# Token sums of a mixture-of-experts stage split over three places of TensorE's order, on Trainium2

## What is computed

```python
def block_mlp(args):
    xb, e = args
    return (jax.nn.silu(xb @ w_gate[e]) * (xb @ w_up[e])) @ w_down[e]
...
y_pad = y_pad * w_pad[:, None].astype(y_pad.dtype)
out = jax.ops.segment_sum(y_pad, tok_pad, num_segments=n_tok)
```

## Time and profile before

| | |
|---|---|
| median of three runs | 2187.53 us (2187.5 to 2188.99) |
| the profiled execution | 2186.75 us, span 2184.9 us |
| TensorE busy over the span | 2123.9 us (97%) |
| VectorE busy | 1211.1 us (55%) |
| ScalarE busy | 855.5 us (39%) |
| mean granted TensorE clock | 0.995 of full speed |
| from the first matmul of expert 0's `gate_up` to that of expert 31's | from 1709.33 us to 2156.12 us |

### The profile page before, as it was taken

One profiled execution on the slowest core, in us unless ns is written; L12 is line 12 of the kernel. 1 busy time (PEld: TensorE's weight loads), 2 busy tenths in 40 slices (PEclk: granted clock), 3 DMA queues, 4 the chain that ended last, 5 costly groups with the idle time before them and its releaser, 6 DMA issues.

```text
span 2184.9 us, 29571 instructions
## 1 busy us (share of the span) xinstructions
PE 2123.9 (97%) x12238; PEld 1521.8 (70%) x12238; DVE 1211.1 (55%) x1983; ACT 855.5 (39%) x1385; POOL 221.1 (10%) x301
## 2 busy tenths in 40 slices
PE   7999999999999999999999999999999899999998
PEld 6868757877777777898888888888867433333333
DVE  3532972439888867875423466345443445544454
ACT  4325461468886544672332542334443111111112
POOL 2000000013331022562000000000001000000000
PEclk9999999999999999999999999999999999999999
DMA  7122112423322444201222221433446899999994
GB/s 249 59 74 93 46 39 83 127 87 97 97 77 94 164 127 154 92 22 41 94 80 97 97 97 40 135 108 123 135 174 243 330 420 420 420 420 420 421 420 194
DMA packets 115703, 366.60 MB, mean 168 GB/s; under 512 B 7952, under 2 KB 36944, under 8 KB 90352
## 3 DMA queue, kind: packets, MB, share of 16 engines
q1 hardware_dynamic: 105888, 329.34, 40.2%
q0 software_dynamic: 9168, 29.00, 3.9%
q10 hardware_dynamic: 512, 6.34, 0.7%
HBM read 358.44 MB, written 10.54 MB: 169 GB/s over the span
## 4 chain that ended last, share of the span: by engine, by line
PE 88%; DVE 8%; ACT 2%; issue 1%; DMA 0%; POOL 0%; SPq 0%; DVEq 0%; ACTq 0%; POOLq 0%
PE bank L956 39%; PE bank L1167 13%; PE bank L1711 10%; PE bank L1725 5%; PE bank L1733 3%; PE bank L1284 2%; PE bank L1180 2%; PE bank L1211 2%; DVE resid L3369 2%; PE bank L1276 1%; PE bank L1113 1%; PE bank L1701 1%; PE bank L1104 1%; DVE w_lo L2447 1%; PE bank L1073 1%
## 5 line engine op out<-in xcount | busy, mean ns | idle before, releaser
L2447 DVE TENSOR_TENSOR w_lo<-raw,w_hi 128x2048 fp32r<-128x2048 f32 x117 | 268.6, 2296 | 444.1 <-ACT w_hi L1842 443.9
L1842 ACT ACTIVATE w_hi<-raw 128x2048 fp32r<-128x2048 f32 x117 | 223.9, 1914 | 393.9 <-PE bank L956 357.5
L3369 DVE TENSOR_TENSOR resid<-bank,resid 128x512 f32<-128x512 f32 x244 | 151.1, 680 | 182.6 <-PE bank L1733 182.6
L956 PE MATMUL bank<-hT_hi,w_hi 128*128 128x512 f32 x512 | 199.9, 390 | 2.5 <-DVE y_lo L3065 2.3
L956 PE MATMUL bank<-hT_lo,w_hi 128*128 128x512 f32 x512 | 199.2, 389 | 0.0
L956 PE MATMUL bank<-hT_hi,w_lo 128*128 128x512 f32 x512 | 199.2, 389 | 0.0
L1711 PE MATMUL bank<-piece,xT 128*64 128x512 f32 x792 | 183.4, 592 | 0.0
L1167 PE MATMUL bank<-hT_hi,w_hi 128*128 128x512 f32 x432 | 173.9, 402 | 0.9 <-DVE hT_lo L2511 0.9
L1167 PE MATMUL bank<-hT_hi,w_lo 128*128 128x512 f32 x432 | 168.2, 389 | 0.0
L1167 PE MATMUL bank<-hT_lo,w_hi 128*128 128x512 f32 x432 | 168.1, 389 | 0.0
L1711 PEld LDWEIGHTS bank<-piece,xT 128*64 128x64 f32 x792 | 59.5, 137 | 118.8 <-issue 118.8
(11 more groups left out here) (625 smaller groups left out, 4166.8 us busy)
## 6 DMA issues: line engine op xcount, KB each, us to landing
piece<-expert_w_gate SPq DMA_DIRECT2D x52, 1024.0 KB, 19.0
piece<-expert_w_down SPq DMA_DIRECT2D x49, 1024.0 KB, 19.2
piece<-expert_w_up SPq DMA_DIRECT2D x47, 1024.0 KB, 20.6
raw<-w_in SPq DMA_DIRECT2D x40, 1024.0 KB, 5.1
raw<-even_w_in SPq DMA_DIRECT2D x18, 1024.0 KB, 5.2
raw<-odd_w_in SPq DMA_DIRECT2D x16, 1024.0 KB, 5.6
raw<-expert_w_gate SPq DMA_DIRECT2D x12, 1024.0 KB, 16.8
raw<-expert_w_up SPq DMA_DIRECT2D x12, 1024.0 KB, 18.9
```

Source lines behind the costliest of these rows:

```text
L956: mm = pe.matmul(out, st, mv, start=first and x == 0, stop=last and x == 2)
L1842: act.activation(split_to(m)[0][:], raw[n % RAW][:], ACT.Copy).then_inc(sem("hi_done"), 1)
L2447: dve.tensor_tensor(split_to(m)[1][:], raw[split_of[m] % RAW][:], f32(split_to(m)[0][:]), ALU.subtract).then_inc(sem("lo_done"), 1)
L3369: dve.tensor_tensor(r, psum[bank][:], r, ALU.add).then_inc(sem(name), 1)
```

## The change

The sums of an expert's result are taken apart over its successor's turn. Those of token tiles 0 and 1 are issued inside `gate_up`, after its first half (f = 3). That of tile 2 stands directly behind `gate_up`, that of tile 3 behind `acts_T`. On VectorE the two adds of tile 2 move in front of `pair_out`; those of tile 3 stay behind it. This holds for turns 1 to 30. The number of instructions is the same.

```diff
+    IN_GATE_UP, AFTER_GATE_UP = (0, 1), (2,)
...
-        def gate_up(w, x, arrived):
+        def gate_up(w, x, arrived, between=()):
...
                 if f % 4 == 3:
                     mm.then_inc(sem("gu_used"), 1)
+                if f == 3:
+                    for old, t in between:
+                        sum_rows(old, t)
...
-            gate_up([piece(e, k) for k in range(PIECES)], xT, lambda k: pe.wait_ge(*piece_in(e, k)))
+            summed_now = 0 < e < NE - 1
+            gate_up([piece(e, k) for k in range(PIECES)], xT, lambda k: pe.wait_ge(*piece_in(e, k)),
+                    [(e - 1, t) for t in IN_GATE_UP] if summed_now else ())
...
             elif e:
-                sum_rows(e - 1, 0)
-                sum_rows(e - 1, 1)
+                for t in AFTER_GATE_UP:
+                    sum_rows(e - 1, t)
...
             elif e:
-                sum_rows(e - 1, 2)
-                sum_rows(e - 1, 3)
+                sum_rows(e - 1, NT - 1)
...
             dve.wait_ge(sem("e_silu"), e + 1)
             product()
+            if 0 < e < NE - 1:
+                added_rows(e - 1, (2,))
             if e + 1 < NE:
                 dve.wait_ge(sem("x_T"), (e + 1) // 2 + 2 if e else 2)
                 dve.wait_ge(sem("gu_used"), 2 * e + 2)
                 pair_out(e + 1)
             if 0 < e < NE - 1:
-                added_rows(e - 1, (2, 3))
+                added_rows(e - 1, (3,))
```

## The result

| | before | after |
|---|---|---|
| median of ten runs each | 2189.38 us (2185.94 to 2192.17) | 2194.93 us (2191.31 to 2196.45) |
| ratio | | 1.0023, 95% interval 1.0015 to 1.0031 |
| profiled execution | 2186.75 us | 2196.45 us |
| its first matmul of `gate_up`, expert 0 | 1709.33 us | 1714.07 us |
| `down` of expert 0 to `down` of expert 30 (turns 1 to 30) | 432.62 us | 437.56 us |

A forecast was written before the change was run, and what follows sets the result against it. TensorE's order was taken as the bound. Even turns 2.47 + 1.27 - 3.97 = -0.23 us, odd 3.35 + 1.27 - 3.98 = +0.64 us, fifteen each: +6.2 us on 2187.53 us, 2193.7 us; range 2188.0 to 2200.0 us.

The forecast's parts named there:

- TensorE's order is the bound, transfers are not: Expert loop: TensorE's order sets the time; transfers would bind only after a gain of over 10 us.
- The two kinds of turn must be costed apart: Turns 1 to 30: fifteen even turns at -0.23 us each, fifteen odd turns at +0.64 us each.
- The insertion costs 1.27 us: Two tiles' sums inside `gate_up` add 1.27 us to each of turns 1 to 30, bounded by 0.92 and 1.67 us.
- The three small differences of rounded times: Around the inserted sums: entering 0.09 us, coming back 0.05 us, outer steps 0.10 us longer than the inner ones.
- The rivals with 0.92 to 1.21 us and with 1.67 us: Cheaper insertion in `gate_up`, no change, chance 0.26; insertion laying weight loads bare, 2205.7 us, chance 0.06.
- The sign that I gave for it: Step from the 8th pair of `gate_up` through the sums to the 9th: 1.70 us; wrong if under 1.6 us.
- From the first sum behind gate_up to acts_T 0.86 us in the even turn: Even turn: 0.86 us with one tile's sum in between, bounded by ScalarE's copy.
- From acts_T to down 1.61 us: Hand-over to `down` in both kinds of turn: 1.61 us, the middle of 1.65 and 1.58 us.
- Costed at nothing: Tile 2's adds ahead of `pair_out`, waits for `ey_lo` and emptied banks, and the weight transfers' queue cost nothing.
- Clock: Rival: TensorE's granted clock falls to 1.2 GHz, +14 us for a single turn so hit, 2208 us; chance 0.02.
- The range: Whole kernel: 2188.0 to 2200.0 us, an insertion of 1.08 to 1.48 us.
- the case of no change: Rival: insertion in `gate_up` of 0.92 to 1.21 us, even and odd turns nearly cancel; chance 0.26.

The follow-up runs named there:

- x_one_even: Kernel before, but in even turns tile 0's sum inside `gate_up`, tile 1's directly behind it; odd turns unchanged. Ratio 0.9977 to before; turns 1 to 30 426.86 us.
- x_even: The change in even turns only, old order in odd turns; 14.17 us even, 14.43 us odd, ratio 0.9987 to before.
- x_odd: The change in odd turns only, old order in even turns; 14.42 us even, 14.99 us odd, +8.62 us against before.
- x_split: Against the change, tile 0's sum after f = 3 and tile 1's after f = 5; 14.53 us even, 15.34 us odd, +15.38 us against before.
- x_vector: Kernel before with only the adds of tile 2 moved ahead of `pair_out` on VectorE; both turns 14.42 us, -0.03 us against before.
- x_one: Against the change, only tile 0 inside `gate_up`, tile 1 behind it, tiles 2 and 3 behind the transposes, VectorE's old order; 14.04 us even, 14.65 us odd.
- x_late: Against the change, tiles 2 and 3 both behind the transposes, nothing directly behind `gate_up`; 14.31 us even, 14.46 us odd.

## Why the prediction was right

It said 2193.7 us, +6.2 us on the median it knew, and slower. The measured ratio gives +5.0 us, and the mechanism is the one it named. That 2194.93 us lies only 1.2 us from 2193.7 us is in part luck: with seven more runs the median before rose from 2187.53 to 2189.38 us, while the forecast of the change was too large by 1.2 us. Point by point, in its own order:

- **TensorE's order is the bound, transfers are not.** Right. In the profiles the stage's length follows TensorE's steps and waits to hundredths of a microsecond, and the share and rate of the transfers are the same in both. x_one_even, 5.76 us shorter, shows no wait for a transfer either.
- **The two kinds of turn must be costed apart.** Right, and it carries the sign: -0.24 us even (forecast -0.23), +0.57 us odd (forecast +0.64). x_even and x_odd show each alone.
- **The insertion costs 1.27 us.** 1.27 us in odd and 1.29 us in even turns. The three small differences of rounded times were real: entering 0.10 us (3.54 against 3.44 us), coming back 0.05 us, longer outer steps 0.10 us each, as x_split shows by paying them twice. The rivals with 0.92 to 1.21 us and with 1.67 us are out. The sign that I gave for it, 1.70 us from the 8th pair to the 9th, came out at 1.67 us (the 8th pair starts at 1947.38 + 3.60 - 0.59 = 1950.39 us, the 9th at 1952.06 us). It should have been 1.65 us, since the 0.05 us of coming back lie behind the 9th pair and do not belong in that step.
- **From the first sum behind gate_up to acts_T 0.86 us in the even turn.** 1956.50 - 1955.64 = 0.86 us.
- **From acts_T to down 1.61 us.** This term was too large. It is 1958.09 - 1956.50 = 1.59 us in the even turn and 1943.90 - 1942.37 = 1.53 us in the odd one. I took the middle between turn 0, where the product started 0.10 us after ScalarE had ended, and the last turn, where it started after 0.03 us. In the two turns read here it started after 0.02 and 0.03 us. In the odd turn the transposes stand behind others of their shape and are done sooner: `silu_g` starts 0.63 us after their start where it is 0.70 us in the even turn. The two values give 15 x 0.08 + 15 x 0.02 = 1.5 us less. The insertion of 1.29 us in even turns gives 0.3 us more, the steps in front of the odd `acts_T` (1.73 us, forecast 1.74) 0.15 us less. That makes 4.8 us in place of 6.2 us, and 4.94 us were measured; the rest is rounding of single steps.
- **Costed at nothing.** x_vector confirms it for VectorE's new order. `ey_lo` was ready in time: it was done at 1948.32 + 0.75 = 1949.07 us, the inserted sums start at 1950.92 us, and no wait stands ahead of them.
- **Clock.** The granted clock is 1.00, the 2.4 GHz level, in every window from 1723 to 2156 us, with waits of 0.27 us ahead of `down` and groups of sums cycling through four banks. The oscillation that the Trainium skill, "TensorE: Matmul & The Clock Gate", section "A second HAM failure mode: psum-queue depth-cycling", tells of did not show.
- **The range.** It was said to leave out the lower third of the case of no change. By its own terms that case is an insertion of 0.92 to 1.21 us and the range begins at 1.08 us, so it leaves out rather more than half of it. The chances did not depend on it.

The sum's size was near the bound of what runs can tell, and the chances said so. It is the turns, 15 of each kind in every profile, that settle it.

## What to carry to other kernels

Work that fills a wait is free only where it stands. Before moving it to relieve another engine, price it at its new place: its own steps, and the passages between matmul shapes on both sides of it. Where a loop's turns have the same length, check whether they have it for the same reason: here odd turns were full on TensorE and even ones waited for VectorE, and the gain lay in treating them apart and in moving only as much as frees the waiting engine.

## What the runs showed of the hardware

I had not expected how exactly the steps add: the three new orders x_split, x_one and x_late gave turns that differ from the sums of single steps, written down ahead, by at most 0.03 us. The change's own odd turn missed its sum by 0.07 us, for the hand-over that was taken too long. A passage from column-split matmuls of `gate_up` to row-split sums and back costs 0.35 us beyond the matmuls themselves, at the 2.4 GHz level of the clock. And the stretch ahead of the experts, the same code in all, varies by 5.5 us over nine executions; why it does is open, and I made no run for it.
